# A hybrid decoder step on one core: the last expert pair's slot weights by an indirect gather, the second pair's gate buffers refilled in halves

## Chip, cores and metric

The kernel runs on one core of one Trainium2 chip. The metric is device time in microseconds, the median of several executions. The profile is of one further execution. The core has five engines that run their own instruction streams: PE (TensorE), DVE (VectorE), ACT (ScalarE), POOL (GpSimd) and SP (SyncE), which here only issues DMAs. Sixteen DMA engines move the data of all queues.

## What is computed

One layer step for 512 prompt tokens and 8 sample tokens (520 in all), in float32, width 1024:

```python
z = rms_norm(x) @ w_in                     # q, k, v, B, C, u
attn = dilated windows over q, k, v        # 12 heads of 64, windows (128,1) (512,4) (2048,16)
conv = B * conv3_causal(C * u)
h = x + concat(rms_norm(attn), rms_norm(conv)) @ w_out
t = rms_norm(h)
# hierarchical mixture of experts
g   = argmax(t @ w_router_group)                       # 1 of 4 groups
top2 of the 8 experts of g, w_sel = softmax(top_v) * p_g
y   = h + sum over the 2 chosen experts e of w_sel[e] * (silu(t @ wg[e]) * (t @ wu[e])) @ wd[e]
```

Each of the 32 experts has w_gate and w_up of 1024 x 256 and w_down of 256 x 1024, 3 x 1 MB, so 101 MB of weights are read once. Each token has two choices, 1040 in all.

## The kernel before

**Stages.** First comes the input projection with norm and rotary, then the sample tokens' attention with the caches, the prompt's attention, the output projection together with the router (it ends near 348 us), and then the experts, two at a time.

**The expert stage.** The 32 experts are worked in 16 pairs (`PAIRS`). A pair has 128 slots, 64 for each expert (`SL`). Which token sits in which slot is computed by the router stage: `in_slot` marks for each of the two choices and each tile of tokens the slot of each token, `in_pair` the pair. The product `tabulate` on PE turns these into `tbl`: `tbl[:, 0, i]` is the token in each slot of pair i, `tbl[:, 1, i]` the choice (2 x token + which of the two). A slot that is empty holds a number beyond the bound.

For pair i, POOL gathers the tokens' rows by an indirect DMA from `hn_rows` (L2255), PE turns them (`turn_tokens`, L1139), DVE copies them out with the norm gain (`tokens`), PE makes gate and up in one bank (`pair`, L1129, 32 matmuls), ACT and DVE make silu(gate) * up (`inner`, `hidden`), PE turns that and multiplies by the down weights (`pair_down`, L1147 and L1156, 16 matmuls), ACT and DVE copy half of the result each, and POOL scatters the rows by choice into `results` in DRAM (L2263). At the end the rows are read back by token and summed with the weights `w12` of the two choices.

**The last pair is different.** Its rows are not scattered. ACT scales them by `last_weight`, the weight of the choice in each slot, while it copies them out of the bank (`weighted_row`, L1469), and PE adds them to their tokens' rows with a 0/1 matrix (`holder`, L1201). `last_weight` is made by `weigh` (L1031 to L1038): ten matmuls with `in_slot` as stationary operand and one moving column each (`weigh_by`, the choice weights of the last pair), which PE does between pair 0's down product and pair 1's gates. ACT waits for it before it copies out pair 1, and DVE copies the column out in pair 0.

**Weights.** Three slots (`WSLOTS`) of the ring in SBUF hold the weights of three pairs. SP refills a slot in order: `expert(a, b, s, i)` waits until the gates of pair i - 3 are done (`gu_done`), issues four DMAs of 1 MB (`gates`, L533; 128 rows of 8 KB), waits until the down product of that pair is done (`dn_done`), and issues two DMAs of 1 MB (`downs`, L546). Two refills are done in halves by `half_gates` (L541): eight DMAs of 512 KB, 128 rows of 4 KB each. They are those of experts 6 and 7 into slot 0, whose first half starts when PE is half way through pair 0's gates (`pair_half`), and those of the last pair, 30 and 31. SP's queue, like every engine's stream, is worked strictly in order. Each of PE, ACT and DVE peels a few pairs and then loops; on PE the pairs 1 to 12 are four turns of a loop of three.

Of the kernel before, what the change touches and what calls it, by code (L numbers as in the profile page):

```python
# [56 lines left out]
def ds(i, n):  # L57
    return bass.ds(i, n)
# [68 lines left out]
def build(nc, x_prompt, x_sample, cache_k, cache_v, state_conv, g_norm_mix, w_in, g_q, g_k, w_conv, g_attn_out,  # L127
# [3 lines left out]
    with ctx:  # L131
# [6 lines left out]
        hn_rows = nc.dram_tensor("hn_rows", [TOK, D], F32, kind="Internal").ap()  # L138
        results = nc.dram_tensor("results", [CHOICES, D], F32, kind="Internal").ap()
        table = nc.dram_tensor("table", [TABLE, 2], U32, kind="Internal").ap()  # L140
        q_rows = nc.dram_tensor("q_rows", [DEC, DA], F32, kind="Internal").ap()
# [114 lines left out]
        def sm(name):  # L256
# [39 lines left out]
        last_token, last_weight = st[:, 146:147], st[:, 147:148]  # L296
        weigh_by = st[:, 148:158].rearrange("p (k t) -> p k t", k=2)
        w12 = st[:, 130:140].rearrange("p (k t) -> p k t", k=2)

# [5 lines left out]
            ssc_std conv_std state_turned conv_turned conv_evac conv_out  # L305
            q_out scores_s turned_s soft_in soft_done probs_turned probs_placed v_used pv_s head_done
            gathered_s attn_s_done
            s_done masked exp_done p_turned p_evac_a p_evac_v o_done o_evac
            a_squared a_std a_turned a_evac opp_done op_done op_evac opp_evac h_done
            h_root h_scaled h_turned h_evac r_done r_evac   # L310
            r_exp r_sub assign count_done count_read addr_done list_done scattered slot_ready tbl_done tbl_ready ov_in
            xg_turned xg_evac gu_done silu_done act_done ht_done ht_evac dn_done dn_evac_a dn_evac_v 
# [118 lines left out]
        def _(sp):  # L431
# [66 lines left out]
            sp.wait_ge(S["z_summed"], summed(1, NT))  # L498
            sp.dma_start(q_rows, qs[0:DEC, :]).then_inc(S["q_out"], 16)
            wload(5)  # L500
# [77 lines left out]
            sp.wait_ge(S["pair_half"], 1)  # L578
            half_gates((6, 7), 0, 0, gu_in[0])
            sp.wait_ge(S["gu_done"], 1)  # L580
            half_gates((6, 7), 0, 1, gu_in[0])
            sp.wait_ge(S["dn_done"], 1)
            downs((6, 7), 0)
            expert(8, 9, 1, 4)
            expert(10, 11, 2, 5)
# [48 lines left out]
        def _(pe):  # L634
# [394 lines left out]

            def weigh():  # L1030

                pe.wait_ge(S["tbl_ready"], 3)
                pe.wait_ge(S["count_read"], len(GROUPS))
                for m in range(T5):
                    for i in range(2):
                        last = pe.matmul(bank[7][:, 0:1], in_slot[:, i, m, :], weigh_by[:, i, m:m + 1],
                                         start=(m == 0 and i == 0), stop=(m == T5 - 1 and i == 1))
                last.then_inc(S["tbl_done"], 1)  # L1038


            def out_group(m, g):
# [72 lines left out]

            def pair(i, s, turn, first, split=False):

                if not first:
                    pe.wait_ge(S["silu_done"], i)
                    pe.wait_ge(S["act_done"], i)
                pe.wait_ge(S["xg_evac"], 2 * i + 1)  # L1120
                loads = 64 * turn if first or s > 0 else 64 * turn + 64
                pe.wait_ge(*((S["front_in"], 80) if split else (gu_in[s], loads)))
                for k in range(KD):
                    if k == KD // 2:
                        pe.wait_ge(S["xg_evac"], 2 * i + 2)
                        if split:
                            pe.wait_ge(gu_in[s], loads)
                    for h in range(2):
                        last = pe.matmul(bank[2][64 * h:64 * h + 64, :], xgT[:, k, 64 * h:64 * h + 64],  # L1129
                                         gate_up[s][h][:, :, k, :], start=(k == 0), stop=(k == KD - 1))  # L1130
                    if first and k == KD // 2 - 1:
                        last.then_inc(S["pair_half"], 1)
                last.then_inc(S["gu_done"], 1)
# [27 lines left out]


            pair(0, 0, 1, True)
            turn_tokens(1, 1, 16)
            pair_down(0, 0, 1, True)
            weigh()
            with pe.Fori(0, 4) as j:
                for n, s in enumerate((1, 2, 0)):
                    i = 3 * j + 1 + n
                    turn = j + 1 + (1 if s == 0 else 0)  # L1170
                    pair(i, s, turn, False)
                    turn_tokens(i + 1, (s + 1) % 3, 16 * (j + 1) + (16 if s == 0 else 0))
                    pair_down(i, s, turn, False)
# [44 lines left out]
        def _(act):  # L1218
# [228 lines left out]
            def pair(i, s, turn, first):  # L1447
                inner(i, first)
                if turn is not None:
                    act.wait_ge(res_sem[s], turn)  # L1450
                elif i == 1:
                    act.wait_ge(S["tbl_done"], 2)
                act.wait_ge(S["dn_done"], i + 1)
                act.activation(yo[s][:, 0:512], bank[4][:, :], ACT.Copy).then_inc(S["dn_evac_a"], 1)
# [23 lines left out]

            act.wait_ge(res_sem[0], 80)
            act.wait_ge(S["act_done"], PAIRS)  # L1480
            act.wait_ge(S["pair_half"], 2)
            weighted_row(0)
# [19 lines left out]
        def _(dve):  # L1502
# [5 lines left out]
            dve.memset(eps, EPS)  # L1508
            dve.memset(zero, 0.0)
            dve.memset(xsT, 0.0)  # L1510
            dve.memset(mixsT, 0.0)
# [506 lines left out]
            step(tt(w12[:, 1, :], w12[:, 0, :], e2, ALU.mult))  # L2018
            tt(weigh_by, in_pair[:, :, :, PAIRS - 1], w12, ALU.mult).then_inc(S["tbl_ready"], 1)

# [14 lines left out]
            for i in range(4):  # L2035
                hidden(i, i == 0)
                tokens(i + 1)
                result(i, i % 3, 16 * (i // 3) if i >= 3 else None)
                if i == 0:
                    dve.wait_ge(S["tbl_done"], 2)  # L2040
                    dve.tensor_copy(last_weight, bank[7][:, 0:1])
            with dve.Fori(0, 3) as j:
# [109 lines left out]
        def _(pool):  # L2152
# [11 lines left out]
            def spread_q(b):  # L2164

                if b >= 2:
                    pool.wait_ge(S["scores_s"], b - 1)
                else:
                    pool.wait_ge(S["q_out"], 16)
                pool.dma_start(qb[b % 2], q_rows[b].partition_broadcast(P)).then_inc(qb_in[b % 2], 16)  # L2170
# [100 lines left out]
            for i in range(PAIRS - 1):  # L2271
                if i + 4 < PAIRS:
                    pool.wait_ge(S["xg_turned"], 2 * i + 4)
                    gather((i + 1) % 3, tbl[:, 0, i + 4:i + 5])
                scatter(i, i % 3, tbl[:, 1, i:i + 1])
            for s in range(WSLOTS):
                pool.wait_ge(res_sem[s], 80)
# [9 lines left out]
            with pool.If(more > 0):  # L2287
# [14 lines left out]
                with pool.Fori(0, OV_PAIRS // 3) as j:  # L2302
                    for n, s in enumerate((1, 2, 0)):
# [3 lines left out]
                        for h in range(2):  # L2307
                            row = pool.value_load(ov_list[0:1, 1, ds(k2 + h, 1)], min_val=0, max_val=TABLE - SL)
                            pool.dma_start(idx[h * SL:(h + 1) * SL, s, :], table[ds(row, SL), :]).then_inc(S["ov_in"], 16)
                        pool.wait_ge(S["ov_in"], 32 * (3 * j + n + 1))  # L2310
                        pool.sem_inc(S["moved_go"], 1)
# [31 lines left out]
```

## Time and profile before

| | |
|---|---|
| median of 3 runs | 597.2 us (597.18 to 600.34) |
| the profiled execution's own time | 603.15 us |
| its span, first to last instruction | 601.5 us |
| mean granted TensorE clock | 0.975 of full |
| PE matmul busy | 552.0 us (92%) |
| PE weight load busy | 322.4 us (54%) |
| DVE busy | 278.9 us (46%) |
| ACT busy | 168.3 us (28%) |
| POOL busy | 156.6 us (26%) |
| moved by DMA | 163.48 MB, mean 272 GB/s |

Shares are of the span. A busy share is an average over stages with different limits, so the table does not say what bounds the end; the views by window, by wait and by chain do. In the windows view the DMA share is the mean busy share of the 16 DMA engines; it can exceed 1 a little, since packets overlap.

### The profile page before, as it was taken

The page shows a single profiled execution, that of the slowest core. Times are in us where ns is not written, and L with a number is a line of the kernel's source. Part 1 is how long each engine was busy: PE and PEld are TensorE (multiplying, and loading weights), DVE is VectorE, ACT ScalarE, POOL GpSimd, SP SyncE. Part 2 cuts the span into 40 slices and gives each one's busy share as a digit, 9 for nine tenths or more (in the row PEclk, how much of TensorE's full clock was granted, in tenths as well). Part 3 has the DMA queues.
Part 4 walks back from the last instruction along what each step waited for, and adds up shares of the span by engine and source line. Part 5 has one row for each costly group of instructions (what it writes and reads, how often), then busy time and mean ns, then how long its engine had stood idle before and what let it go on. Part 6 is the DMA issues. An engine that isn't in the chain of part 4 may idle for free.

```text
span 601.5 us, 8410 instructions
## 1 busy us (share of the span) xinstructions
PE 552.0 (92%) x2972; PEld 322.4 (54%) x2972; DVE 278.9 (46%) x694; ACT 168.3 (28%) x386; POOL 156.6 (26%) x187
## 2 busy tenths in 40 slices
PE   6999999999999989999999999999987878789993
PEld 4798899897675655553555944333332223233321
DVE  5887677978314899614458631111210111111245
ACT  7445343423302647622322210100110000000013
POOL 0488788410001187610000021121110111100003
PEclk9999999999999999999999798999998899999998
DMA  7990332589586920049805759999999999999856
GB/s 277 278 289 24 121 145 79 182 250 310 180 210 200 405 104 2 3 138 392 350 35 212 278 177 379 409 420 419 421 422 420 423 417 422 420 421 419 349 225 244
DMA packets 48199, 163.48 MB, mean 272 GB/s; under 512 B 8666, under 2 KB 22042, under 8 KB 36872
## 3 DMA queue, kind: packets, MB, share of 16 engines
q1 hardware_dynamic: 41344, 144.93, 64.1%
q0 software_dynamic: 6528, 17.01, 7.8%
q10 hardware_dynamic: 288, 1.05, 0.4%
q8 instruction: 21, 0.34, 0.2%
q14 instruction: 18, 0.15, 0.1%
HBM read 151.06 MB, written 19.76 MB: 284 GB/s over the span
## 4 chain that ended last, share of the span: by engine, by line
PE 47%; DMA 16%; SPq 11%; DVE 7%; issue 3%; POOL 3%; ACT 3%; DVEq 0%; POOLq 0%; ACTq 0%
PE bank L1129 10%; DMA ring<-in_w_up_dram 10%; PE bank L1061 9%; SPq L533 8%; PE bank L1156 4%; DMA x<-q_rows 3%; SPq L546 3%; DMA ring<-results 2%; PE bank L1012 2%; PE bank L831 2%; POOL ring L2188 2%; PE bank L926 2%; PE bank L809 2%; PE bank L832 2%; PE bank L836 2%
## 5 line engine op out<-in xcount | busy, mean ns | idle before, releaser
L1129 PE MATMUL bank<-ring,work 128*64 128x512 f32 x512 | 121.2, 629 | 18.3 <-DMA ring<-in_w_up_dram 18.3
L1129 PEld LDWEIGHTS bank<-ring,work 128*64 128x64 f32 x512 | 39.7, 144 | 96.5 <-issue 82.4
L1506 DVE TENSOR_TENSOR work<-work,bank 128x256 f32<-128x256 f32 x16 | 6.7, 421 | 135.1 <-ACT work L1441 135.1
L752 PE MATMUL bank<-split 128*128 128x384 f32 x192 | 66.1, 344 | 0.1
L1156 PE MATMUL bank<-ring,work 128*64 128x512 f32 x256 | 58.5, 598 | 7.6 <-ACT work L1445 7.6
L753 PE MATMUL bank<-split 128*128 128x384 f32 x192 | 64.3, 335 | 0.0
L2255 POOL DMA_INDIRECT work<-hn_rows,tbl x15 | 15.2, 1016 | 107.7 <-PE bank L1139 92.4
L1441 ACT ACTIVATE work<-bank 128x256 f32<-128x256 f32 x16 | 6.1, 384 | 131.1 <-PE bank L1129 131.1
L1061 PE MATMUL bank<-ring 128*128 128x512 f32 x96 | 42.6, 595 | 0.0
L2188 POOL TENSOR_TENSOR ring<-ring 128x192 f32<-128x192 f32 (+1 forms) x40 | 38.8, 989 | 7.9 <-DVEq L1601 6.8
L2263 POOL DMA_INDIRECT results<-work,tbl x15 | 15.0, 1001 | 99.0 <-DVE work L2033 99.0
L1506 DVE TENSOR_TENSOR split<-ring,split 128x768 fp32r<-128x768 f32 (+1 forms) x35 | 37.5, 1105 | 6.1 <-PE bank L739 6.0
L783 PE MATMUL bank<-split 128*128 128x384 f32 x192 | 37.8, 338 | 0.5 <-DVE split L1506 0.5
L752 PEld LDWEIGHTS bank<-split 128*128 128x128 f32 x192 | 36.1, 188 | 3.3 <-issue 2.4
L1156 PEld LDWEIGHTS bank<-ring,work 128*64 128x64 f32 x256 | 17.0, 136 | 38.8 <-issue 27.4
L1362 ACT ACTIVATE ring<-ring,st 128x512 f32<-128x512 f32 (+3 forms) x48 | 26.6, 554 | 37.6 <-DVE st L1680 37.5
L753 PEld LDWEIGHTS bank<-split 128*128 128x128 f32 x192 | 36.1, 188 | 0.0
L2033 DVE COPY work<-bank 128x512 f32<-128x512 f32 x15 | 10.4, 692 | 52.9 <-PE bank L1156 52.9
L783 PEld LDWEIGHTS bank<-split 128*128 128x128 f32 x192 | 33.4, 188 | 1.7 <-DVE split L1506 1.0
L1061 PEld LDWEIGHTS bank<-ring 128*128 128x128 f32 x96 | 17.8, 190 | 20.6 <-issue 20.6
L1915 DVE SCALAR_TENSOR_TENSOR x<-bank,st,x 128x512 f32<-128x512 f32 (+1 forms) x20 | 14.9, 747 | 25.9 <-PE bank L1061 25.2
L1241 ACT ACTIVATE split<-ring 128x768 fp32r<-128x768 f32 x32 | 25.1, 833 | 3.1 <-DMA ring<-in_w_in_dram 3.1
(277 smaller groups left out, 873.2 us busy)
## 6 DMA issues: line engine op xcount, KB each, us to landing
ring<-in_w_down_dram SPq DMA_DIRECT2D x32, 1024.0 KB
ring<-in_w_gate_dram SPq DMA_DIRECT2D x28, 1024.0 KB
ring<-in_w_up_dram SPq DMA_DIRECT2D x28, 1024.0 KB
ring<-in_w_in_dram SPq DMA_DIRECT2D x7, 1536.0 KB, 11.3
results<-work POOLq DMA_DIRECT2D x1, 4160.0 KB, 24.5
x<-in_x_prompt_dram SPq DMA_DIRECT2D x8, 512.0 KB, 15.7
ring<-in_w_out_dram SPq DMA_DIRECT2D x2, 2048.0 KB, 16.1
ring<-in_w_gate_dram SPq DMA_DIRECT2D x8, 512.0 KB, 20.6
```

Source lines behind the costliest of these rows:

```text
L533: sp.dma_start(gate_up[s][h][:, o, :, :], w[0, ds(e, 1)].rearrange("e (p k) f -> p (e k) f", p=P)).then_inc(gu_in[s], 16)
L546: sp.dma_start(down[s][h], w_down[0, ds(e, 1)].rearrange("e (p k) n -> p (e k) n", p=P)).then_inc(dn_in[s], 16)
L752: pe.matmul(bank[n % 3][:, 0:CW], xT_high[:, k, cols], w_high[c][:, k, :], start=(k == 0), stop=False)
L753: pe.matmul(bank[n % 3][:, 0:CW], xT_low[:, k, cols], w_high[c][:, k, :], start=False, stop=False)
L783: last = pe.matmul(bank[n % 3][:, 0:CW], xT_high[:, k, cols], w_low[c][:, k, :], start=False, stop=(k == KD - 1))
L1061: last = pe.matmul(bank[g][:, :], src, wout[g % 2][:, k, :], start=(k == rng[0]), stop=(k == rng[-1]))
L1129: last = pe.matmul(bank[2][64 * h:64 * h + 64, :], xgT[:, k, 64 * h:64 * h + 64], gate_up[s][h][:, :, k, :], start=(k == 0), stop=(k == KD ...
L1156: last = pe.matmul(bank[4 + j][64 * h:64 * h + 64, :], hT[:, c, 64 * h:64 * h + 64], down[s][h][:, c, j * 512:(j + 1) * 512], start=(c == ...
L1241: act.activation(w_high[c][:, 2 * i:2 * i + 2, :], wchunk[c][:, 2 * i:2 * i + 2, :], ACT.Copy)\
L1362: act.activation(buf, buf, ACT.Exp, bias=nmax[:, u % 4:u % 4 + 1], scale=-1.0, accum_out=den[:, u % 24:u % 24 + 1]).then_inc(S["exp_done"], 1)
L1506: return dve.tensor_tensor(out, a, b, op)
L2188: last = pool.tensor_tensor(sv[:, :, a * half:(a + 1) * half], zv[:, :, b * half:(b + 1) * half], bc(rope_g[2 * (cc // 2) + 1][0:w, t, a * ...
```

## The change

The weights of the last pair's slots are no longer computed by PE. Instead SP writes `w12` to a small DRAM tensor `weights` (one row of 4 bytes for each choice; a token's two choices lie beside each other, so each DMA row has 8 bytes), in five DMAs, one for each tile of tokens, behind the first halves of the gates of 6 and 7. POOL reads the last pair's slots from it by one indirect DMA (128 rows of 4 bytes) after the scatter of pair 2, indexed by `tbl[:, 1, PAIRS - 1]`. Empty slots keep the 0 of a memset. `w12` is stored with the two choices of a tile side by side. `weigh` and its waits on ACT and DVE go. The second refill of slot 1 (experts 8 and 9) is done in halves, as that of slot 0 before it: the first half when PE is half way through pair 1's gates, the second when they are done. On PE the pairs 1 to 3 stand outside the loop, which has three turns left.

```diff
+        weights = nc.dram_tensor("weights", [CHOICES, 1], F32, kind="Internal").ap()
...
-        weigh_by = st[:, 148:158].rearrange("p (k t) -> p k t", k=2)
-        w12 = st[:, 130:140].rearrange("p (k t) -> p k t", k=2)
+        w12 = st[:, 130:140].rearrange("p (t k) -> p k t", k=2)
...
@@ SP @@
             half_gates((6, 7), 0, 0, gu_in[0])
+            sp.wait_ge(S["tbl_ready"], 3)
+            for m, t in enumerate(ORDER):
+                n = TILES[t]
+                sp.dma_start(weights[2 * t * P:2 * (t * P + n), :].rearrange("(t k) o -> t (k o)", k=2), w12[0:n, :, m])\
+                    .then_inc(S["staged"], 16)
             sp.wait_ge(S["gu_done"], 1)
             half_gates((6, 7), 0, 1, gu_in[0])
             sp.wait_ge(S["dn_done"], 1)
             downs((6, 7), 0)
-            expert(8, 9, 1, 4)
+            sp.wait_ge(S["pair_half"], 2)
+            half_gates((8, 9), 1, 0, gu_in[1])
+            sp.wait_ge(S["gu_done"], 2)
+            half_gates((8, 9), 1, 1, gu_in[1])
+            sp.wait_ge(S["dn_done"], 2)
+            downs((8, 9), 1)
             expert(10, 11, 2, 5)
@@ PE @@
-            def weigh():
-                pe.wait_ge(S["tbl_ready"], 3)
-                pe.wait_ge(S["count_read"], len(GROUPS))
-                for m in range(T5):
-                    for i in range(2):
-                        last = pe.matmul(bank[7][:, 0:1], in_slot[:, i, m, :], weigh_by[:, i, m:m + 1],
-                                         start=(m == 0 and i == 0), stop=(m == T5 - 1 and i == 1))
-                last.then_inc(S["tbl_done"], 1)
...
-                loads = 64 * turn if first or s > 0 else 64 * turn + 64
+                loads = 64 * turn if apart or s == 2 else 64 * turn + 64
...
-                    if first and k == KD // 2 - 1:
+                    if apart and k == KD // 2 - 1:
                         last.then_inc(S["pair_half"], 1)
...
-            pair(0, 0, 1, True)
+            pair(0, 0, 1, True, apart=True)
             turn_tokens(1, 1, 16)
             pair_down(0, 0, 1, True)
-            weigh()
-            with pe.Fori(0, 4) as j:
+            for i in range(1, 4):
+                s = i % 3
+                pair(i, s, i // 3 + 1, False, apart=(i == 1))
+                turn_tokens(i + 1, (s + 1) % 3, 16 * (i // 3 + 1))
+                pair_down(i, s, i // 3 + 1, False)
+            with pe.Fori(0, 3) as j:
@@ ACT @@
-                elif i == 1:
-                    act.wait_ge(S["tbl_done"], 2)
...
+            act.wait_ge(S["few_in"], 16)
@@ DVE @@
+            dve.memset(last_weight, 0.0)
...
-            tt(weigh_by, in_pair[:, :, :, PAIRS - 1], w12, ALU.mult).then_inc(S["tbl_ready"], 1)
+            dve.engine_nop().then_inc(S["tbl_ready"], 1)
...
-                if i == 0:
-                    dve.wait_ge(S["tbl_done"], 2)
-                    dve.tensor_copy(last_weight, bank[7][:, 0:1])
@@ POOL @@
                 scatter(i, i % 3, tbl[:, 1, i:i + 1])
+                if i == 2:
+                    pool.wait_ge(S["staged"], 16 + 16 * (NT + 1))
+                    pool.indirect_dma_start(last_weight, None, weights, bass.IndirectOffsetOnAxis(tbl[:, 1, PAIRS - 1:PAIRS], 0),
+                                            bounds_check=CHOICES - 1, oob_is_err=False).then_inc(S["few_in"], 16)
```

## Rows read from the trace of the kernel before

**Rows 1.** The profile's page, the span in 40 slices of 15.04 us: GB/s moved.
```profile
GB/s 277 278 289 24 121 145 79 182 250 310 180 210 200 405 104 2 3 138 392 350 35 212 278 177 379 409 420 419 421 422 420 423 417 422 420 421 419 349 225 244
```
**Rows 2.** Windows: stretch, its length, busy time (instructions) by engine, clock, DMA share, GB/s.
```profile
400.00:420.00 20.00, 19.32 (x94) 6.86 (x92) 3.00 (x5) 1.96 (x4) 3.02 (x3) 1.00 1.02 421
```
**Rows 3.** Waits of PE, 415 to 560 us: engine, line, releaser, total, times, longest.
```profile
PE bank L1129 <- DMA ring<-in_w_up_dram: 18.3, 8, 4.4
```
**Rows 4.** The chain that ended last: start, length, what.
```profile
527.85 28.45 DMA ring<-in_w_up_dram
556.44 7.09 PE bank L1129 x32
```
**Rows 5.** Windows, where the stream of weights pauses.
```profile
372.00:373.00 1.00, 1.00 (x9) 0.79 (x8) 0.53 (x2) 0.38 (x1) 0.00 (x0) 1.00 0.51 213
373.00:374.00 1.00, 0.52 (x5) 0.28 (x6) 1.00 (x2) 0.38 (x1) 0.18 (x1) 1.00 0.77 156
```
**Rows 6.** Timeline of SP's DMA issues: start, length, line, what.
```profile
353.27 0.64 SPq L541 DMA_DIRECT2D ring<-in_w_up_dram  x1
355.38 0.33 SPq L541 DMA_DIRECT2D ring<-in_w_gate_dram  x1
...
361.01 0.86 SPq L546 DMA_DIRECT2D ring<-in_w_down_dram  x2
372.05 0.33 SPq L533 DMA_DIRECT2D ring<-in_w_gate_dram  x1
```
**Rows 7.** Timeline of PE.
```profile
346.01 2.32 PE L1025 MATMUL bank<-work 128*128 128x32 f32 x20
...
360.90 2.39 PE L1036 MATMUL bank<-st,work 128*128 128x1 f32 x20
363.22 8.78 PE L1129 MATMUL bank<-ring,work 128*64 128x512 f32 x32
...
377.41 7.04 PE L1129 MATMUL bank<-ring,work 128*64 128x512 f32 x32
```
**Rows 8.** Windows at the start of pair 1's gates.
```profile
363.00:364.00 1.00, 1.00 (x7) 0.64 (x8) 0.16 (x1) 0.00 (x0) 0.61 (x1) 0.82 1.03 406
364.00:365.00 1.00, 1.00 (x4) 0.25 (x3) 0.00 (x0) 0.00 (x0) 0.00 (x0) 0.50 1.01 406
```
**Rows 9.** Windows where a queue of weights drains.
```profile
298.00:299.00 1.00, 1.00 (x3) 0.38 (x2) 0.86 (x5) 0.00 (x0) 0.00 (x0) 1.00 0.27 107
299.00:300.00 1.00, 1.00 (x5) 0.46 (x4) 0.93 (x9) 0.00 (x0) 0.00 (x0) 1.00 0.04 16
...
566.00:567.00 1.00, 1.00 (x8) 0.34 (x6) 0.57 (x3) 0.00 (x0) 0.00 (x0) 1.00 0.89 365
570.00:571.00 1.00, 1.00 (x6) 0.29 (x4) 0.00 (x0) 0.00 (x0) 0.26 (x1) 1.00 0.43 180
```
**Rows 10.** Windows while the last pair's half gates are moved.
```profile
548.00:549.00 1.00, 0.84 (x6) 0.40 (x4) 1.00 (x3) 0.12 (x1) 0.00 (x0) 1.00 1.01 422
550.00:551.00 1.00, 1.00 (x6) 0.28 (x4) 0.00 (x0) 0.00 (x0) 0.00 (x0) 1.00 0.99 410
```
**Rows 11.** A window while slot 0's half gates are moved.
```profile
355.00:356.00 1.00, 1.00 (x9) 0.73 (x8) 0.13 (x1) 0.38 (x1) 0.00 (x0) 1.00 0.98 299
```
**Rows 12.** Timeline of POOL.
```profile
349.49 1.11 POOL L2255 DMA_INDIRECT work<-hn_rows,tbl  x1 [14.69 <-DVE tbl L1998]
...
352.22 0.99 POOL L2255 DMA_INDIRECT work<-hn_rows,tbl  x1 [0.30 <-issue]
```
**Rows 13.** Timeline of DVE: the last of the router weights' instructions.
```profile
350.85 0.17 DVE L1506 TENSOR_TENSOR st<-work,st 128x10 f32<-128x10 f32 x1
```
**Rows 14.** Windows in which the router's weights are loaded.
```profile
25.00:26.00 1.00, 1.00 (x13) 0.51 (x15) 1.00 (x2) 0.00 (x0) 1.00 (x1) 1.00 1.17 298
26.00:27.00 1.00, 1.00 (x13) 0.31 (x6) 1.00 (x2) 0.00 (x0) 1.00 (x2) 1.00 1.28 160
```
**Rows 15.** The window in which the conv outputs are stored.
```profile
259.00:260.00 1.00, 1.00 (x4) 0.52 (x5) 0.17 (x2) 0.94 (x4) 0.00 (x0) 1.00 0.04 8
```

More of the change, by code:

```diff
@@ L305, in build @@
             ssc_std conv_std state_turned conv_turned conv_evac conv_out
-            q_out scores_s turned_s soft_in soft_done probs_turned probs_placed v_used pv_s head_done
+            staged scores_s turned_s soft_in soft_done probs_turned probs_placed v_used pv_s head_done
             gathered_s attn_s_done
@@ L310, in build @@
             h_root h_scaled h_turned h_evac r_done r_evac
-            r_exp r_sub assign count_done count_read addr_done list_done scattered slot_ready tbl_done tbl_ready ov_in
+            r_exp r_sub assign count_done count_read addr_done list_done scattered slot_ready tbl_done tbl_ready few_in
             xg_turned xg_evac gu_done silu_done act_done ht_done ht_evac dn_done dn_evac_a dn_evac_v
@@ L498, in _ @@
             sp.wait_ge(S["z_summed"], summed(1, NT))
-            sp.dma_start(q_rows, qs[0:DEC, :]).then_inc(S["q_out"], 16)
+            sp.dma_start(q_rows, qs[0:DEC, :]).then_inc(S["staged"], 16)
             wload(5)
@@ L1112, in _, with pair @@
                 tabulate(b)
-            def pair(i, s, turn, first, split=False):
+            def pair(i, s, turn, first, split=False, apart=False):
                 if not first:
@@ L1160, in pair_down @@
                 last.then_inc(S["dn_done"], 1)
-            pair(0, 0, 1, True)
+            pair(0, 0, 1, True, apart=True)
             turn_tokens(1, 1, 16)
             pair_down(0, 0, 1, True)
-            weigh()
-            with pe.Fori(0, 4) as j:
+            for i in range(1, 4):
[4 more added lines that the diff above has]
+            with pe.Fori(0, 3) as j:
                 for n, s in enumerate((1, 2, 0)):
-                    i = 3 * j + 1 + n
-                    turn = j + 1 + (1 if s == 0 else 0)
+                    i = 3 * j + 4 + n
+                    turn = j + 2 + (1 if s == 0 else 0)
                     pair(i, s, turn, False)
-                    turn_tokens(i + 1, (s + 1) % 3, 16 * (j + 1) + (16 if s == 0 else 0))
+                    turn_tokens(i + 1, (s + 1) % 3, 16 * (j + 2) + (16 if s == 0 else 0))
                     pair_down(i, s, turn, False)
@@ L1479, in _ @@
             act.wait_ge(res_sem[0], 80)
+            act.wait_ge(S["few_in"], 16)
             act.wait_ge(S["act_done"], PAIRS)
-            act.wait_ge(S["pair_half"], 2)
+            act.wait_ge(S["pair_half"], 3)
             weighted_row(0)
@@ L2168, in spread_q @@
                 else:
-                    pool.wait_ge(S["q_out"], 16)
+                    pool.wait_ge(S["staged"], 16)
                 pool.dma_start(qb[b % 2], q_rows[b].partition_broadcast(P)).then_inc(qb_in[b % 2], 16)
@@ L2308, in _ @@
                             row = pool.value_load(ov_list[0:1, 1, ds(k2 + h, 1)], min_val=0, max_val=TABLE - SL)
-                            pool.dma_start(idx[h * SL:(h + 1) * SL, s, :], table[ds(row, SL), :]).then_inc(S["ov_in"], 16)
-                        pool.wait_ge(S["ov_in"], 32 * (3 * j + n + 1))
+                            pool.dma_start(idx[h * SL:(h + 1) * SL, s, :], table[ds(row, SL), :]).then_inc(S["few_in"], 16)
+                        pool.wait_ge(S["few_in"], 32 * (3 * j + n + 1) + 16)
                         pool.sem_inc(S["moved_go"], 1)
```

## The prediction

> **What bounds the kernel now.** I read the profile in this order: the slices of DMA rate, the waits of the expert stage, the chain, and then one-microsecond windows of the few places that the change touches.
>
> The change sits in the expert stage, which begins near 348 us. From the slice that starts at 376 us until 556 us the rate stays at 409 to 423 GB/s [rows 1], and in a 20 us window of that stretch the 16 DMA engines are busy with a share of 1.02 at 421 GB/s [rows 2]. From 415 us to 560 us PE waits 18.3 us in all, 8 times, for expert weights to land [rows 3]. The chain agrees: the gate matmuls of pair 14, at 556.44 us, start when a weight DMA lands (28.45 us of chain for that DMA), and from there the chain runs over pair 14 to the stores [rows 4]. So the end of the kernel hangs on the end of one long stream of weights. PE work saved at 361 us is worth only what it lets the stream gain. Where does the stream not run? In two windows the DMA share falls to 0.51 and 0.77, from 372 us to 374 us [rows 5]; everything asked for had landed, and the gates of experts 8 and 9 are issued only when PE has ended pair 1's gate matmuls: the issue at 372.05 us follows the L1129 matmuls that end at 372.0 [rows 6, 7].
>
> **The change part by part.** *1. The ten-matmul product goes.* `weigh` is 2.39 us of PE between pair 0's down product and pair 1's gates (360.90 to 363.22 us) [rows 7]; with it goes one DVE copy, which nothing on PE's side waits for. Pair 1's gates then take 8.78 us, where pair 2's take 7.04 for the same 32 matmuls. The granted clock is 0.82 in the first microsecond and 0.50 (the 1.2 GHz level) in the second; before the fall PE ran the 1-column product, and the 32-column product at 346.01 us is followed by gates at 1.00 all the same [rows 7, 8]. I take it that without the 1-column product the clock holds; then pair 1's gates run from 360.9 to 367.9 us. If it does not hold, they end at 369.7. Both are before the stream runs dry, so the choice moves nothing in the sum. Nothing else keeps pair 1 back: its tokens are copied out by DVE under pair 0's down product, and its weights were loaded under the output projection.
>
> *2. The gates of 8 and 9 in two halves.* The first half can be issued half way through pair 1's gates, at about 364.4 us, the second at 367.9 (369.7 at the low clock), against 372.05 now. The queue then holds more work at the moment when it now runs empty, and the gap of 372 to 374 closes. The size of the gap: against 421 GB/s the two windows of 213 and 156 GB/s lack 208 + 265 = 473 KB, or 1.1 us of the whole stream [rows 2, 5]. That is the upper bound. The lower bound is 0: the 16 engines do not run dry together. Where the queue drained before, the share was 0.27 and then 0.04 in the last two microseconds, and at the very end of the weights it tapers for long (still 0.43 at 570, where the full stream ended near 566) [rows 9]. A matmul waits for the last engine, and the last engine may have had work through most of the gap. I take half, 0.6 us. The Trainium skill, page "DMA: Bandwidth & Descriptors", section "Latency and other measured facts", says that engines 7 and 15 are usually slower than the others. By it the gap on the engines that count is worth nothing, and the sum would come out 0.6 us later; the taper agrees that some lag, and no row says which.
>
> The halves have rows of 4 KB where whole gates have 8 KB. The last pair's gates are loaded in the same halves, and in windows where these are in transit the rate is 422 and 410 [rows 10], 416 in the mean, against 421: on 8 x 0.524 = 4.19 MB that is 10.07 instead of 9.95 us, so 0.1. The other halves in the trace, for slot 0, ran at 299 GB/s with a share of 0.98 at 355 us [rows 11], together with three gathers issued from 349.49 to 352.22 [rows 12]. By that row 4.19 MB would take 14.0 us, 4.0 more. I take the first, since at 370 us the queue is full and only one gather is near, as at 550; both ends stay for the range.
>
> *3. The weights are written to DRAM by rows of 8 bytes.* Four DMAs of 128 rows and one of 8: 520 tiny packets on SP's queue, 32 or 33 to an engine. SP reaches them after the first halves for slot 0, whose last issue ends at 353.9 us, and its new wait (the router weights ready) is over by then: the last instruction of that DVE chain is at 350.85 us [rows 6, 13]. Behind the wait stand the second halves for slot 0, then the downs, then everything. Issuing takes 5 x 0.45 us (from the shortest to the longest issue here, 0.33 to 0.64, with the step to the next) [rows 6], up to 356.2 us, so the second halves leave 0.8 us later than 355.38. The cover: the first halves and three gathers, 2.1 MB and some 0.8, at 299 GB/s keep the engines busy for over nine microseconds from 352, until about 361 us. SP may stand at a full queue there, but a full queue is one that feeds the engines. Cost of the issuing: 0, and 0.8 us if the cover were gone.
>
> What the packets take from the stream is shown by no row of such writes. From below: at 25 and 26 us some 2048 small packets of the router's weights pass (rows of 16 and 128 bytes), and the rate is 298 and 160 at full share [rows 14]; (123 + 261) KB / 421 = 0.9 us for 2048, so 0.2 us for 520. From above: the conv outputs, ten rows of 1 KB to DRAM, show a share of 0.04 in their microsecond [rows 15], 0.04 x 16 / 10 = 64 ns of engine time a row, latency included; 520 x 64 / 16 = 2.1 us. The writes will pass in a full queue as the rows of 25 us did, where latency is hidden, so I go near the low end: 0.4 us. The same page of the Trainium skill (section "Specifications") says that transfers under 512 B make the DMA engine read, modify and write. No run here shows a duration of that; by it these writes would cost more than reads of the same size and the upper row would be the nearer one, which is the second rival below.
>
> *4. The gather of the last pair's weights.* One POOL instruction like the others, 1.0 to 1.1 us [rows 12], behind the scatter of the third pair, where POOL is idle until the next pair's tokens are turned; 128 packets of 4 bytes add 8 to an engine, under 0.1 us by the low row. Thirteen pairs pass before ACT uses it. Its waits on the staging DMAs are long over. Cost: 0; if POOL were busy, 1.0 us on a queue whose gathers run two pairs ahead.
>
> *5. The rest.* A 1-column memset at the start lies under the first loads. The router weights in another order are the same small DVE instructions, 0.17 us [rows 13]. Three pairs of PE code stand outside the loop, and ACT and DVE lose a wait that was never the last. Cost 0, bound by one such instruction, 0.2 us, either way.
>
> **Sum.** -0.6 (gap) + 0.4 (520 writes) + 0.1 (4 KB rows) = -0.1 us on the profiled execution's own 603.15 us (span 601.5). That execution is 1.0% above the median of 597.2 us; I carry the difference over unscaled: 597.1 us. Own range of this case, from -1.1 + 0.2 to 0 + 0.4 + 0.5, with 0.6 for what two medians may differ by: 595.7 to 598.7.
>
> **The rivals.** *A, the PE time comes through.* Pair 1 ends 2.3 us (product) + 1.8 us (clock) earlier and every refill after it too; if the stream outside the profiled run is faster than in it, it runs dry more often and follows PE: -4.1 us, 593.1 us. For it: all the waits of PE for weights lie behind 415 us. Against it: a share of 1.02 over that same stretch [rows 2], and 18.3 us of waits that would only grow [rows 3].
>
> *B, the 8-byte writes are dear.* 2.1 us instead of 0.4, in the middle of the full queue: -0.6 + 2.1 + 0.1 = +1.6 us, 598.8 us, and more if a write of 8 bytes takes longer than one of 1 KB. For it: the only writes of short rows to DRAM that stand alone in the trace [rows 15]. Against it: that row was taken in an idle queue.
>
> *C, slower: the 4 KB rows run at 299 GB/s.* 14.0 instead of 10.0 us for gates 8 and 9, in a stream without slack: -0.6 + 0.4 + 4.0 = +3.8, 601.0 us. It decides as soon as the halves run below 390 GB/s (4.19 MB / 0.390 = 10.7 us, which with the writes eats the gap). For it [rows 11]; against it [rows 10].
>
> *D, the change does not do what it says:* SP is still busy with other issues when the half mark comes, and the gap stays. SP issues nothing between 361.87 and 372.05 us now [rows 6], so this needs the staging to hold it for over ten microseconds: 0.4 + 0.1 = +0.5, 597.7 us.
>
> **How the numbers follow.** Forecast 0.62, A 0.13, B 0.13, C 0.08, D 0.04. About 3 us (0.5%) is what a measurement of this kernel can tell from no change, since three runs lie between 597.18 and 600.34. Faster by over that: A, 0.13. Slower: C and the dearer quarter of B, 0.11. Within: 0.76. The range leaves out C, that quarter of B and the lower half of A, some 0.18: 593.0 to 600.0 us.
>
> **What would show it.** Right: no PE product of 1-column matmuls; pair 1's gates from about 361 to 368 us at clock 1.0; gate DMAs of slot 1 near 364.4 and 368; no window from 362 to 550 us with a DMA share under 0.9; pair 14's gates within a microsecond of 556.4. A would show as pair 14's gates near 552. B as a dip of the rate between 354 and 363 us below the 299 of now, and a stream that ends 2 us later. C as 300 GB/s for some ten microseconds after 371. The forecast is wrong if pair 14's gates start over 1.5 us from where they start now, or if the part behind them changes its length of 45 us.

## The result and the profile after

| | before | changed |
|---|---|---|
| median, 20 runs each | 599.59 us (597.18 to 602.38) | 601.25 us (599.09 to 604.51) |
| ratio | | 1.0035 (1.0019 to 1.0051) |
| profiled execution, its span | 603.15, 601.5 us | 601.94, 600.3 us |
| start of pair 0's gates | 348.25 us | 348.36 us |
| start of pair 14's gates | 556.44 us | 557.95 us |
| from the one to the other | 208.19 us | 209.59 us |
| from pair 14's gates to the end | 45.06 us | 42.35 us |

The changed kernel is slower by about 2 us. The two profiled executions alone would say the opposite, since the one of before was 3.6 us above its median and the other only 0.7. The profiles of the experiments show that the part from pair 14's gates to the end varies between 41.6 and 45.1 us, and the start of the expert stage between 344.4 and 348.4. I therefore read each profile by the stretch between the start of pair 0's gates and that of pair 14's, which holds most of the weight stream and nothing of either. It has a weakness of its own: pair 14's gates do not always start on a weight that lands. They do in the profile of before [rows 4]; in the changed kernel's they follow PE's own work without a wait:
```profile
557.95 7.09 PE L1128 MATMUL bank<-ring,work 128*64 128x512 f32 x32
```
So beside the stretch stands a count of the stream itself, "landed": the microseconds from the start of pair 0's gates until 60 MB have arrived in packets of 4 KB and more on SP's queue, from the packet records of the trace. It is 167.3 us in the profile of before and 170.0 in the changed kernel's.

PE did what was forecast. Timeline of PE, changed kernel, to be held against [rows 7]:
```profile
348.36 7.09 PE L1128 MATMUL bank<-ring,work 128*64 128x512 f32 x32
...
360.91 7.04 PE L1128 MATMUL bank<-ring,work 128*64 128x512 f32 x32
...
373.34 7.04 PE L1128 MATMUL bank<-ring,work 128*64 128x512 f32 x32
```
Pair 1's gates run at full clock from 360.91 us, and pair 2's start 4.07 us earlier than in [rows 7]. The DMA issues, against [rows 6]:
```profile
353.38 0.89 SPq L541 DMA_DIRECT2D ring<-in_w_up_dram  x1
354.31 2.49 SPq L583 DMA_DIRECT2D weights<-st  x5
356.84 0.70 SPq L541 DMA_DIRECT2D ring<-in_w_gate_dram  x1
...
361.12 0.80 SPq L546 DMA_DIRECT2D ring<-in_w_down_dram  x2
364.55 0.33 SPq L541 DMA_DIRECT2D ring<-in_w_gate_dram  x1
```
The five staging DMAs take SP 2.49 us, and the first half for slot 1 leaves at 364.55, as worked out. What is new is in the stream. Windows of the changed kernel (the last two columns are DMA share and GB/s):
```profile
361.00:362.00 1.00, 1.00 (x8) 0.34 (x6) 0.69 (x1) 0.60 (x1) 0.00 (x0) 1.00 1.16 331
362.00:363.00 1.00, 1.00 (x6) 0.29 (x4) 0.00 (x0) 0.00 (x0) 0.29 (x1) 1.00 1.98 250
363.00:364.00 1.00, 1.00 (x8) 0.38 (x6) 0.00 (x0) 0.00 (x0) 0.72 (x1) 1.00 0.92 98
364.00:365.00 1.00, 1.00 (x8) 0.34 (x6) 0.00 (x0) 0.00 (x0) 0.00 (x0) 1.00 0.72 98
365.00:366.00 1.00, 1.00 (x6) 0.29 (x4) 0.00 (x0) 0.00 (x0) 0.00 (x0) 1.00 0.62 107
366.00:367.00 1.00, 1.00 (x8) 0.37 (x6) 0.00 (x0) 0.00 (x0) 0.00 (x0) 1.00 0.77 119
372.00:373.00 1.00, 1.00 (x8) 0.38 (x6) 0.00 (x0) 0.00 (x0) 0.00 (x0) 1.00 1.06 442
```
The pause at 372 us is gone: 442 GB/s in the window that had 213 [rows 5]. Instead the rate is near 100 GB/s for four microseconds from 363, with the engines busy 0.6 to 0.9 of the time. The packet records show what comes ahead of that. The 520 packets of 8 bytes start between 359.97 and 362.00 us, behind the first halves and the gathers, and 9 ns are recorded for each. The slow packets are the ones behind them: in the four microseconds from 362.00 only 92 weight packets of 4 KB start, of 446 ns in the mean, up to 2.5 us; at the same distance from pair 0's gates the kernel before has 333, of 160 ns. Waits of PE from 415 to 560 us, against [rows 3]:
```profile
PE bank L1128 <- DMA ring<-in_w_up_dram: 22.3, 8, 4.7
```
4.0 us more than before. From pair 2's gates to pair 14's PE takes 184.6 us, where it took 179.0. These 5.6 us are the 4.07 gained at the front and the 1.5 by which pair 14 starts later; 4.0 of them are waits for weights, and most of the rest is matmuls that took longer: PE is busy for 156.0 us of the way, 154.4 before.

### The profile page after: what moved, and what is told of

Same layout as the page of the kernel before. It is cut to its first block, busy times and chain, and to the rows that moved or that the text cites. A ratio compares the mean times of both kernels' runs of the same rounds, so it can differ in the third digit from the quotient of the medians.

```text
span 600.3 us, 8367 instructions
## 1 busy us (share of the span) xinstructions
PE 548.3 (91%) x2952; PEld 319.0 (53%) x2952; DVE 278.4 (46%) x693; ACT 168.0 (28%) x386; POOL 157.3 (26%) x188
## 4 chain that ended last, share of the span: by engine, by line
PE 54%; SPq 17%; DMA 7%; DVE 5%; issue 3%; ACT 3%; POOL 1%; DVEq 0%; POOLq 0%; ACTq 0%
SPq L533 12%; PE bank L1060 9%; PE bank L1128 8%; SPq L546 5%; DMA ring<-in_w_up_dram 5%; PE bank L1155 4%; PE bank L793 4%; PE bank L762 3%; PE bank L763 3%; PE bank L1022 2%; PE bank L936 2%; PE bank L819 2%; PE bank L841 2%; PE bank L842 2%; PE bank L846 2%
```

## The experiments

Each kernel was timed in five rounds beside the kernel before (12 executions, 6 for the doubled staging), one excepted that says so; a ratio compares with the kernel before in the same session. "Stretch" is the time from pair 0's gates to pair 14's in its one profile, "landed" the count told above. Rates are those of the eight microseconds from 361 us. Pair 0's gates start at 347.8 to 348.4 us in some profiles and up to 3.8 us earlier in others, so these windows do not all show the same piece of the stream; where that matters, the rate at the changed kernel's distance (12.64 us behind the start of pair 0's gates) is given too.

**Halves alone.** The change to SP, and on PE the loop and the half mark that go with it, applied to the kernel before:
```diff
-            expert(8, 9, 1, 4)
+            sp.wait_ge(S["pair_half"], 2)
+            half_gates((8, 9), 1, 0, gu_in[1])
+            sp.wait_ge(S["gu_done"], 2)
+            half_gates((8, 9), 1, 1, gu_in[1])
+            sp.wait_ge(S["dn_done"], 2)
+            downs((8, 9), 1)
```


> The kernel before with only the refill of experts 8 and 9 in halves (the product weigh stays where it was). Theory W (the 520 writes of 8 bytes to DRAM cost the stream some 4.5 us, all else gives a little): 0.5 to 1.1 us faster than before, no window under 0.9 DMA share from 362 to 550 us, pair 14's gates at 555.3 to 556.0. Rival H (the halves are the loss, rows of 4 KB or a worse order of transfers): 2 us or more slower, with a rate near 300 GB/s for some ten microseconds from 372.

Measured: 596.78 us, ratio 0.9958 (0.9928 to 0.9988), stretch 204.70. Faster by about 2.5 us, more than the 1.1 that I gave the pause at most. Landed: 165.9 us, 1.3 us earlier than in the first profile of the kernel before. While the halves are moved the rate is far from 300 GB/s, so rival H and my rival C fall (windows, this kernel):
```profile
369.00:377.00 8.00, 7.52 (x40) 2.89 (x38) 2.31 (x4) 1.36 (x3) 1.02 (x1) 1.00 1.01 401
```
Whole gates at the same distance gave 421 and 424 GB/s (the two profiles with the product moved and the refill whole, below), but by 60 MB they are at most 0.4 us ahead.

**No staging.** The changed kernel without the block of five DMAs and without the gather.

> The changed kernel without the five writes and without the gather of the weights; last_weight stays 0, so the last pair's rows are added with weight 0. Theory W: the rate from 361 to 369 us is above 300 GB/s throughout, the kernel is 4 to 5 us faster than the changed one and 1.5 to 3 us faster than before. Rival H: within 1 us of the changed kernel. Rival T (the end of the kernel, not the stream, changed its length): pair 14's gates start with those of the changed kernel and the time does not move.

Measured: 598.04 us, ratio 0.9990 (0.9965 to 1.0016), stretch 206.59. 2.7 us faster than the changed kernel by the ratios, 3.0 by the stretch; that is less than expected, though the rate is full again. The first window is that of 361 us, the second the one at the changed kernel's distance:
```profile
361.00:369.00 8.00, 7.52 (x40) 2.89 (x38) 1.62 (x3) 0.77 (x2) 1.50 (x2) 1.00 1.03 421
358.75:366.75 8.00, 8.00 (x43) 2.98 (x39) 1.28 (x3) 0.98 (x2) 1.01 (x1) 1.00 1.02 412
```
Against the changed kernel's 197 GB/s (below) the second is (412 - 197) x 8 KB = 1.7 MB, 4.1 us of the stream at 421. The stream keeps that loss: landed is 165.9 us here and 170.0 in the changed kernel, 4.1 apart. The stretch shows only 3.0 of it; pair 14's gates start on no weight in either profile. Rival T falls.

**Staging done twice.** The block in a loop over two DRAM tensors:
```diff
-            for m, t in enumerate(ORDER):
+            for into in (weights, weights_b):
+                for m, t in enumerate(ORDER):
```


> The changed kernel with the 520 writes done twice, the second time into a second DRAM tensor that nobody reads. Theory W: 3.5 to 5.5 us slower than the changed kernel, the low rate (about 100 GB/s) holds for about nine microseconds instead of four. Rival H and rival T: under 0.5 us slower.

Measured: 606.20 us, ratio 1.0130 (1.0088 to 1.0172), stretch 214.24, landed 175.2: 5.7 us above the changed kernel by the ratios, 4.6 by the stretch, 5.2 by the landed bytes. Of all edits this is the clearest. Eight microseconds of almost nothing follow, with a share of 0.60:
```profile
361.00:369.00 8.00, 7.52 (x40) 2.87 (x38) 1.62 (x3) 0.77 (x2) 1.51 (x2) 1.00 0.60 47
```

**The same rows to SBUF.** Where does the price arise, at the packet or at its target?
```diff
-                sp.dma_start(weights[2 * t * P:2 * (t * P + n), :].rearrange("(t k) o -> t (k o)", k=2), w12[0:n, :, m])\
-                    .then_inc(S["staged"], 16)
+                sp.dma_start(st[0:n, 148 + 2 * m:150 + 2 * m], w12[0:n, :, m]).then_inc(S["staged"], 16)
```


> The changed kernel with the same 520 rows of 8 bytes copied from SBUF to SBUF instead of to DRAM, in the same place of the same queue, and no gather (last_weight stays 0). If the price is that of a write of 8 bytes to DRAM (theory W, form one): as fast as the kernel without the writes, within 1 us. If the price is that of a small packet wherever it goes (form two): as slow as the changed kernel, and the low rate shows again from 361 us.

Measured: 598.31 us, ratio 0.9991 (0.9965 to 1.0018), stretch 205.03. Form one. The small packets themselves take little of the stream. At the changed kernel's distance the rate is 376 GB/s against 412, 0.7 us; by the landed bytes (166.1) it is 0.3. The window from 361 us:
```profile
361.00:369.00 8.00, 7.77 (x40) 2.92 (x36) 1.41 (x4) 0.69 (x3) 1.02 (x1) 1.00 1.03 381
```

**The product moved, halves kept.** On the kernel with the halves:
```diff
             pair_down(0, 0, 1, True)
-            weigh()
...
                 turn_tokens(i + 1, (s + 1) % 3, 16 * (i // 3 + 1))
+                if i == 1:
+                    weigh()
                 pair_down(i, s, i // 3 + 1, False)
```


> The kernel before with the refill of 8 and 9 in halves and weigh moved on PE: behind pair 1's gates and the turning of pair 2's tokens, ahead of pair 1's down product. It has the halves and the early gates of the changed kernel and none of its small DMAs. Theory W (the stream is the bound, PE's order is nothing): as fast as the halves alone, within 1 us, 1.5 to 3.5 us faster than before. Rival A (earlier PE work comes through): 2 to 4 us faster than the halves alone.

Measured: 596.76 us, ratio 0.9953 (0.9925 to 0.9982), stretch 204.91. The same as the halves alone (landed 165.6). Earlier PE work is worth nothing beside them: rival A falls.

**Gather without halves.** The changed kernel with `expert(8, 9, 1, 4)` back.

> The changed kernel with the refill of 8 and 9 whole again, issued when pair 1's gates are done. Theory W: the writes hold the queue until about 369 us, so the whole refill issued at 368 still finds it full: within 1 us of the changed kernel, 1.5 to 3 us slower than before. If the halves are of use beside the writes too, 1 us or more slower than the changed kernel; if they are the loss (rival H), faster than it by 1 us or more.

Measured: 601.30 us, ratio 1.0027 (0.9996 to 1.0059), stretch 209.15, landed 169.9, 196 GB/s. As the changed kernel. Beside the early gates the halves do nothing; the writes do it all.

**520 rows of 512 bytes, and 520 rows of 8 bytes that lie apart.** Both on the kernel without staging; the rows are written to `wide`, a DRAM tensor of [520, 128]:
```diff
+                sp.dma_start(wide[t * P:t * P + n, :], ident[0:n, :]).then_inc(S["staged"], 16)    # rows of 512 bytes
+                sp.dma_start(wide[t * P:t * P + n, 0:2], w12[0:n, :, m]).then_inc(S["staged"], 16) # 8 bytes, 512 apart
```


> The changed kernel with 520 rows of 512 bytes (of a constant tile) written to a DRAM tensor, instead of 520 rows of 8 bytes, in the same place; no gather, last_weight stays 0. If the price comes from the rows being short (under 512 bytes): 0.27 MB, under 1 us slower than without the writes, and no window near 100 GB/s. If it is a price per row written to DRAM: as slow as the changed kernel, 2 to 3 us slower than without.

> The changed kernel with the 520 rows of 8 bytes written to addresses 512 bytes apart instead of side by side; no gather, last_weight stays 0. If the price is that of short rows as such: as slow as the changed kernel, 2 to 3 us slower than without the writes. If it comes from 64 neighbours that lie within the same 512 bytes: under 1 us slower than without the writes, and no window near 100 GB/s.

Measured: 597.15 us, ratio 0.9969 (0.9940 to 0.9998), stretch 206.60, landed 166.8; and 597.98 us, ratio 0.9961 (0.9933 to 0.9990), stretch 205.53, landed 166.2. Neither the row written to DRAM nor the short row has the price by itself; it comes with short rows side by side. Two more distances, by the second dimension of `wide` (16, then 8 floats):

> As the kernel with 520 rows of 8 bytes written 512 bytes apart, but 64 bytes apart; no gather, last_weight stays 0. If the price is one of neighbours in the same 64 bytes: as fast as 512 apart. If it is one of neighbours in the same 512 bytes: a rate of 100 to 200 GB/s for some microseconds from 361 us and 1.5 to 3 us slower than 512 apart.

> As the kernels with 520 rows of 8 bytes written 512 and 64 bytes apart, but 32 bytes apart; no gather, last_weight stays 0. If the price is one of neighbours within 64 bytes: a rate from 361 to 369 us clearly under the 361 GB/s of 64 apart and above the 197 GB/s of side by side, and 0.5 to 2 us slower than 64 apart. If it starts only at closer neighbours (the same 32 bytes): as 64 apart.

Measured: 599.05 us, ratio 1.0012 (0.9984 to 1.0040), stretch 207.23, landed 166.9; and 600.15 us, ratio 0.9993 (0.9969 to 1.0017), stretch 207.44, landed 167.4. The windows, in the order 8 (the changed kernel), 32, 64 and 512 bytes apart:
```profile
361.00:369.00 8.00, 8.00 (x43) 2.98 (x39) 1.28 (x3) 0.98 (x2) 1.01 (x1) 1.00 1.02 197
```
```profile
361.00:369.00 8.00, 7.85 (x40) 2.93 (x36) 1.41 (x4) 0.68 (x3) 1.01 (x1) 1.00 1.00 317
```
```profile
361.00:369.00 8.00, 7.87 (x40) 2.92 (x36) 1.41 (x4) 0.69 (x3) 1.02 (x1) 1.00 1.03 361
```
```profile
361.00:369.00 8.00, 7.81 (x40) 2.93 (x36) 1.41 (x4) 0.69 (x3) 1.01 (x1) 1.00 1.02 381
```
The rate rises step by step. The great step is from 8 to 32; 512 apart is the same as rows to SBUF. By the times 32 and 64 apart can't be told from each other. Neither branch of what I expected of 64 apart came true: there is no rate of 100 to 200 GB/s, and yet the kernel is 3.0 us slower than with 512 apart by the ratios and 1.7 by the stretch (0.7 by the landed bytes). So no distance was found at which the price stops all at once. The distance is not shown to be the cause by itself either: with it grew the piece of DRAM that the 520 rows fill (4, 17, 33 and 266 KB), and no run kept one while it changed the other.

**The changed kernel mended by that.** `weights` becomes [520, 128] and is filled with ones in the idle time of the DMA engines ahead of the expert stage; POOL gathers the token's row and DVE picks one weight of the two:
```diff
-                sp.dma_start(weights[2 * t * P:2 * (t * P + n), :].rearrange("(t k) o -> t (k o)", k=2), w12[0:n, :, m])\
+                sp.dma_start(weights[t * P:t * P + n, 0:2], w12[0:n, :, m])\
...
-                    pool.indirect_dma_start(last_weight, None, weights, bass.IndirectOffsetOnAxis(tbl[:, 1, PAIRS - 1:PAIRS], 0),
-                                            bounds_check=CHOICES - 1, oob_is_err=False).then_inc(S["few_in"], 16)
+                    pool.indirect_dma_start(both, None, weights, bass.IndirectOffsetOnAxis(tbl[:, 0, PAIRS - 1:PAIRS], 0),
+                                            bounds_check=TOK - 1, oob_is_err=False).then_inc(S["few_in"], 16)
```


> The changed kernel made whole with rows that lie apart: weights is [520, 128], filled with ones while the DMA engines are idle before the expert stage, the 520 rows of 8 bytes are written 512 bytes apart, POOL gathers the row of the slot's token, and DVE picks one of its two weights late. If the neighbourhood of the rows is the price: 1.5 to 3.5 us faster than before, 4 to 5 us faster than the changed kernel. If the price needs a reader or was missed before: as slow as the changed kernel.

Measured: 597.68 us, ratio 0.9987 (0.9956 to 1.0017), stretch 205.37, landed 166.2, 392 GB/s. The price is gone with a reader too: 2.9 us below the changed kernel by the ratios (2.0 against its second ratio, below), 4.2 by the stretch, 3.8 by the landed bytes. It does not clearly beat the kernel before; 1.5 to 3.5 us had been expected.

**The product moved, refill whole.** The kernel before with `weigh` later, as in the diff above, and what goes with it: the loop on PE split as in the change, and DVE's copy of the column in pair 1 instead of pair 0.

> The kernel before with weigh moved behind the turning of pair 2's tokens, and the refill of 8 and 9 whole. PE ends pair 1's gates near 368 us, before the stream runs dry at 372. Theory W: either way of issuing earlier closes the pause, so as fast as the kernel with halves and weigh moved, within 1 us, 1.5 to 3.5 us faster than before. If only the halves help: as slow as before.

Measured: 595.98 us, ratio 0.9954 (0.9924 to 0.9985), stretch 205.32, landed 165.8. Once more:

> The kernel before with weigh moved behind the turning of pair 2's tokens, again. Theory W: 1.5 to 3 us faster than before and 3 to 5 us faster than the changed kernel; 205 to 206 us between the gates. If the first ratio of 0.9954 was chance: within 1 us of before.

Measured: 597.85 us, ratio 0.9970 (0.9946 to 0.9995), stretch 204.74, landed 165.6. This simplest edit beats both kernels, in both comparisons: the pause closes if the refill is issued earlier, whether by halves or because PE's product no longer stands ahead of pair 1's gates.

**The kernel before again, and the changed one again.** The first in one round (seven executions are compared), the others in five.

> The kernel before, unchanged, for a second profile. Theory: from the start of pair 0's gates to the start of pair 14's 207 to 209 us (208.2 in the first profile), a pause of the stream at 372 us again, and a part behind pair 14's start of 43 to 45 us, which changes from execution to execution by about 1 us. If the pause of the first profile was chance: no window under 0.9 there.

> The kernel before, unchanged, with as many rounds as the others: shows what a comparison of equals gives here. Expected a ratio between 0.997 and 1.003 and 206.5 to 208.2 us between the starts of the gates of pair 0 and pair 14.

> The changed kernel once more, on one chip with the kernel before as a run of its own and with the kernel whose product is only moved. Theory W (writes +3.9 us, pause -1.8 us in the profiles): 1 to 3 us slower than the kernel before, 209 to 210 us from the start of pair 0's gates to that of pair 14's, and 3 to 5 us slower than the kernel with weigh moved. If the first result was chance: within 1 us of before, 206.5 to 208 us between the gates.

Measured: the kernel before against itself 1.0032 (1.0002 to 1.0062) and 0.9980 (0.9957 to 1.0004), stretches 206.48 and 206.09. The changed kernel 600.75 us, ratio 1.0020 (0.9994 to 1.0046), stretch 209.69. So an interval of these comparisons can be off by 0.3%, and neither 1.0035 nor 1.0020 alone would prove that the changed kernel is slower. That the writes make the stream late is proved by the stretch: 209.15, 209.59 and 209.69 in the three profiles with one set of writes side by side, 206.09, 206.48 and 208.19 in the three of before, and 204.70 to 206.60 in the nine profiles with neither the pause nor writes under 512 bytes apart to DRAM (mean 205.4). Two of before lie within that last range. The landed bytes part the groups better:

| | landed, us |
|---|---|
| the kernel before, three profiles | 167.3, 167.1, 165.9 |
| one set of writes side by side, three | 170.0, 170.2, 169.9 |
| two sets | 175.2 |
| rows 32, 64 bytes apart | 167.4, 166.9 |
| rows 512 bytes apart, two | 166.2, 166.2 |
| rows of 512 bytes; rows of 8 bytes to SBUF | 166.8; 166.1 |
| no such writes and no pause, five | 165.9, 165.9, 165.6, 165.8, 165.6 (mean 165.7) |

How much of this reaches the end of the kernel is less clear. From pair 14's gates to the end the three profiles with the writes take 42.4 us in the mean, the three of before 44.8, so that from pair 0's gates to the end they hardly differ (251.9 and 251.7), while the five without writes and pause take 248.6. Why that last part is longer in the kernel before was not tried. That the changed kernel as a whole is slower than the one before rests on the comparisons: 1.0035 over 20 executions each, 1.0020, and 1.0027 with the refill whole.

The three profiles of before also show what goes with the pause. In the second one the clock fell again behind the 1-column product, the gates took 8.78 us, and the pause stood there:
```profile
362.00:363.00 1.00, 1.00 (x4) 0.24 (x2) 0.00 (x0) 0.00 (x0) 0.00 (x0) 0.50 1.02 406
...
370.00:371.00 1.00, 1.00 (x10) 0.86 (x8) 0.45 (x2) 0.38 (x1) 0.00 (x0) 1.00 0.70 295
371.00:372.00 1.00, 0.52 (x3) 0.20 (x3) 1.00 (x2) 0.38 (x1) 0.11 (x1) 1.00 0.83 147
```
In the third the clock held, pair 1's gates took 7.09 us, and little of the pause was left (its stage starts 3.9 us earlier, so these windows answer to 372 to 374 of the first):
```profile
368.00:369.00 1.00, 0.63 (x4) 0.34 (x6) 0.54 (x1) 0.32 (x1) 0.74 (x1) 1.00 0.93 336
369.00:370.00 1.00, 1.00 (x8) 0.29 (x4) 0.00 (x0) 0.00 (x0) 0.28 (x1) 1.00 0.89 369
```

## Why the prediction was wrong

**The bound** was read rightly in the main. The stream of weights sets the pace; the 4 us that PE gained at the front went into waiting; moving PE work beside the halves changed nothing. That the part behind pair 14 keeps its 45 us was wrong: it varies by 3.5 us.

**The writes: the step that failed.** The term was 0.4 us, between 0.2 and 2.1. Measured: about 4. The stretch with them (mean of three, 209.5) is 4.1 us above that without (205.4), the landed bytes 4.3 (170.0 against 165.7); writing them again added 4.6 by the stretch, 5.2 by the landed bytes and 5.7 by the ratio. Even the upper bound was too low by half, and the range of 595.7 to 598.7 had not even this bound in it: its upper end took the term at 0.4. Both bounds came from rows that lacked what mattered: the small packets of [rows 14] were loads into SBUF, and the rows of [rows 15] were 1 KB long. That the packets pass in a full queue I took as a reason for the low end, and for packets as such this was right (0.3 to 0.7 us for 520 of them, to SBUF or to DRAM 512 bytes apart). Side by side in DRAM they cost 4.1 us x 16 / 520 = 0.13 us of one engine for a row, and not while they are recorded (9 ns each) but behind them, in the weight packets that follow.

I had the mechanism as rival B, with a chance of 0.13 and a price of 2.1. The rule of the Trainium skill that I set beside it ("DMA: Bandwidth & Descriptors", "Specifications": under 512 B a DMA reads, modifies and writes) warned in the right direction. It does not give the price, though: rows of 8 bytes that lie 512 bytes apart fall under it just as much and cost a fifth or less. The dip that I named as its mark, between 354 and 363 us, came at the end of that stretch and behind it, from 362 to 367: the writes, issued from 354.31, started only at 359.97, behind the first halves and the gathers, and the rate fell after them.

**The pause.** The term was 0.6 us, with 1.1 as upper bound. Measured by the landed bytes: 1.5 us in the two profiles of before in which the pause stood (167.2 against 165.7) and 0.1 in the third; by the stretch 206.9 (mean of the three) - 205.4 = 1.5; by the ratios of the kernels with halves or moved product and nothing else 0.3 to 0.5%, 1.8 to 2.8 us, but only 0.6 us in the two without writes to DRAM and without the product (no staging, rows to SBUF). I halved the term because the engines do not run dry together. Nothing of that discount showed where the pause stood, and the slower engines that the Trainium skill names ("DMA: Bandwidth & Descriptors", "Latency and other measured facts"), by which it would have been worth nothing, are not borne out there. Why more comes back than the two windows lack was not tried.

**The clock and the halves.** The clock held without the product, as said: in none of the eleven profiles without it are pair 1's gates slow. That this "moves nothing in the sum" holds for the changed kernel but not for the one before, whose pause is large only when the clock falls. The 4 KB rows cost 0.1 us in the mean by the landed bytes (165.9 and 165.6 with halves, 165.8 and 165.6 with whole gates), which is less than two profiles of one kernel differ by.

**The sum** with the measured terms is -1.5 + 4.1 + 0 = +2.6 us, beside +1.7 between the medians, +2.1 by the ratio and +1.2 in the second comparison. The agreement is rough: the terms are those of the stretch, and the part behind it was 2.4 us shorter with the writes. The forecast of no measurable change rested on two small terms that cancelled; two larger ones of opposite sign did not. Its own signs of being right failed too: the windows from 364 to 367 us have shares of 0.62 to 0.77, and pair 14's gates start 1.5 us late. But signs given as moments are weak in a kernel whose expert stage itself starts up to 4 us earlier or later. The stated range ended at 600.0 and the median is 601.25; 2.4 us of the distance to the forecast is the kernel before itself, which over 20 runs reads 599.59 where three had given 597.2. Three runs were too few to set a range of 7 us by.

## What to carry to other kernels

In a kernel bound by one long DMA stream, 4 KB in 520 rows can cost as much as 1.7 MB (4.1 us at 421 GB/s): look at how many rows a small store has and how near they lie to each other in DRAM, and put them apart (512 bytes was the best distance tried), or keep them out of the stream. A small product on PE that stands ahead of the instruction which frees a buffer is best moved behind it, which here gave 1.8 and 2.8 us by the ratios without any new DMA. And price an operation only from a row that shares its direction, its row length and its spacing; where no such row exists the range must be wide.

## What the hardware showed that I had not expected

- 520 rows of 8 bytes written to DRAM side by side bring a stream of 421 GB/s down to about 100 GB/s for four microseconds (197 over eight); 32, 64 and 512 bytes apart it is 317, 361 and 381 GB/s over the same eight, and with 520 whole rows of 512 bytes, which carry 64 times the data, 405 at the same distance from pair 0's gates, where it is 412 with no such writes. The packets of the writes themselves are recorded with 9 ns each; those behind them are the slow ones. I read this as writes of one neighbourhood that wait for each other and hold up what follows, but no run shows it.
- The granted clock fell to 0.50 right behind the ten 1-column matmuls in four of seven profiles that have them, with the product in its old place (three of four) and moved (one of three), and held in the other three. The same kernel did both.
- A kernel compared with itself over seven executions gave a ratio of 1.0032 whose interval left out 1.
